# Two-block fp32 transformer on one core: keys rotated ahead of a score reading in three head steps, and another order of the first transfers and products

## The reference

```python
h = rmsnorm(x, norm_g)                      # gain norm_g, 1024 wide
proj = h @ w_in                             # queries, keys, values, gates of three branches
# branch A: 4 heads, each the difference of two softmaxes over causal scores (head width 64)
# branch C: 8 heads of width 64, windowed; for 512 tokens with dilations 1, 4, 16, merged by their lse
q, k = partial_rope(q), partial_rope(k)     # first 16 of 64 columns are rotated
s = einsum(q, k) * 64 ** -0.5;  p = softmax(mask(s));  o = p @ v
# branch B: gelu, layernorm, causal token mixing
x = x + (sum over branches of sigmoid(gate) * (y_branch @ w_branch)) @ w_out
```

## Time and profile before

| | us |
|---|---|
| median of 3 runs | 2323.68 |
| lowest, highest | 2322.32, 2325.24 |
| the profiled execution, its own time | 2325.3 |
| its span (first to last instruction) | 2323.5 |
| TensorE busy | 2308.4 |
| VectorE busy | 1481.2 |
| ScalarE busy | 978.6 |

### The profile page before, as it was taken

How to read it: one execution, slowest core, us unless ns; L and a number is a source line. 1 busy time by engine, 2 the same in 40 slices (tenths; PEclk the granted TensorE clock), 3 DMA queues, 4 the chain that set the end, 5 groups by cost and what they waited for, 6 DMA issues and landing times.

```text
span 2323.5 us, 30126 instructions
## 1 busy us (share of the span) xinstructions
PE 2308.4 (99%) x11442; PEld 1881.9 (81%) x11442; DVE 1481.2 (64%) x2781; ACT 978.6 (42%) x1811; POOL 0.2 (0%) x4
## 2 busy tenths in 40 slices
PE   9999999999999999999999999999999999999998
PEld 6888888888888878888877788888887768888887
DVE  6788763435478784444587668566567777658565
ACT  5356542223446553222567543232336764323222
POOL 0000000000000000000000000000000000000000
PEclk9999999999999999999999999999999999999999
DMA  4333334333243333233221133314313112422322
GB/s 167 107 105 105 104 96 112 92 99 100 84 117 109 97 103 114 93 100 117 65 88 55 56 127 102 127 55 145 118 37 97 55 46 100 145 82 91 127 64 99
DMA packets 74766, 226.84 MB, mean 98 GB/s; under 512 B 15296, under 2 KB 16192, under 8 KB 73856
## 3 DMA queue, kind: packets, MB, share of 16 engines
q1 hardware_dynamic: 74336, 224.14, 30.9%
q10 hardware_dynamic: 288, 0.79, 0.1%
HBM read 205.36 MB, written 2.10 MB: 89 GB/s over the span
## 4 chain that ended last, share of the span: by engine, by line
PE 96%; DVE 2%; ACT 1%; issue 0%; DMA 0%; DVEq 0%; SPq 0%
PE bank L590 25%; PE bank L592 25%; PE bank L591 25%; PE bank L2235 2%; PE bank L2237 2%; PE bank L2236 2%; PE bank L1310 2%; PE bank L2054 1%; PE bank L2013 1%; PE bank L1294 1%; PE bank L2038 1%; PE bank L524 1%; PE bank L1283 1%; PE bank L1281 1%; PE bank L2067 1%; PE bank L2096 0%
## 5 line engine op out<-in xcount | busy, mean ns | idle before, releaser
L590 PE MATMUL bank<-h_hi,w_hi 128*128 128x512 f32 x1984 | 784.7, 396 | 0.7 <-DVE sz L1769 0.3
L592 PE MATMUL bank<-h_lo,w_hi 128*128 128x512 f32 x1984 | 773.4, 390 | 0.0
L591 PE MATMUL bank<-h_hi,w_lo 128*128 128x512 f32 x1984 | 773.0, 390 | 0.0
L1157 DVE TENSOR_TENSOR w_lo<-raw_w,w_hi 128x1024 fp32r<-128x1024 f32 x314 | 378.9, 1221 | 97.4 <-ACT w_hi L1145 94.1
L590 PEld LDWEIGHTS bank<-h_hi,w_hi 128*128 128x128 f32 x1984 | 372.7, 188 | 82.5 <-issue 8.3
L592 PEld LDWEIGHTS bank<-h_lo,w_hi 128*128 128x128 f32 x1984 | 372.4, 188 | 79.8
L591 PEld LDWEIGHTS bank<-h_hi,w_lo 128*128 128x128 f32 x1984 | 372.9, 188 | 72.1
L1145 ACT ACTIVATE w_hi<-raw_w 128x1024 fp32r<-128x1024 f32 x314 | 327.6, 1054 | 159.5 <-DMA raw_w<-w_dram 159.1
L2472 ACT ACTIVATE nrm<-bank 128x512 f32<-128x512 f32 x44 | 26.4, 599 | 288.4 <-PE bank L592 288.4
L1611 ACT ACTIVATE ext<-bank 128x512 f32<-128x512 f32 x48 | 28.7, 598 | 274.3 <-PE bank L592 274.3
L1918 DVE TENSOR_TENSOR rope_a<-ext,bank 128x512 f32<-128x512 f32 x32 | 22.0, 688 | 165.8 <-PE bank L592 109.7
(11 more groups left out here) (372 smaller groups left out, 3504.6 us busy)
## 6 DMA issues: line engine op xcount, KB each, us to landing
raw_w<-w_dram SPq DMA_DIRECT2D x312, 512.0 KB, 3.6
down_raw<-w_dram SPq DMA_DIRECT2D x36, 512.0 KB, 4.5
extra_raw<-w_dram SPq DMA_DIRECT2D x10, 512.0 KB, 4.6
k_lo<-k_lo SPq DMA_DIRECT2D x32, 128.0 KB, 2.3
ln_row<-row_dram SPq DMA_DIRECT2D x4, 1024.0 KB, 6.6
last_raw<-w_dram SPq DMA_DIRECT2D x8, 512.0 KB, 4.6
rowp<-row_dram SPq DMA_DIRECT2D x2, 1024.0 KB, 11.9
rot_t<-raw_t SPq DMA_DIRECT2D x128, 16.0 KB
```

Of the source, the lines that this page charges most:

```text
L590: nc.tensor.matmul(dst, lh, rh, start=start, stop=False)
L591: nc.tensor.matmul(dst, ll, rh, start=False, stop=False)
L592: return nc.tensor.matmul(dst, lh, rl, start=False, stop=stop)
L1157: nc.vector.tensor_tensor(lo_of(u), raw_of(u), hi_of(u).bitcast(F32), ALU.subtract) \
```

## The change

Three things. In the steps of the joined heads 4 to 6, VectorE rotates the keys of the next head directly behind its queries, in (a, 1), ahead of the reading of the scores of (a, 2). In (a, 2) nothing is left between the split and `normalise` but the reading of bank O. Head 3's epilogue in (5, 1) then stands behind both rotations. At the start, token block 0 is loaded by SyncE as its third transfer and no longer by ScalarE's queue. And the gain diagonal is made by one instruction and not by two, TensorE makes two full products of zeros ahead of the sums (one and a half before) and none between the sums and the transposes (one before).

```diff
@@ -983,8 +983,7 @@
             sp.dma_start(const[:, 0:2 * P], const_in[:, 0:2 * P]).then_inc(ident_loaded, 16)
             sp.dma_start(colp[:, 0:P1_SUBLN], col_in[0, :, 0:P1_SUBLN]).then_inc(norm_loaded, 16)
             for tb in range(NB):
-                if tb:
-                    sp.dma_start(x[:, tb, :], x_in[tb * P:(tb + 1) * P, :]).then_inc(x_loaded[tb], 16)
+                sp.dma_start(x[:, tb, :], x_in[tb * P:(tb + 1) * P, :]).then_inc(x_loaded[tb], 16)
                 if tb < 2:
                     load(tb)
             load(2)
@@ -1161,18 +1160,17 @@
 
         def gain_sums(pe):
 
+            pe.wait_ge(gain_diag_ready, 1)
             diag = gain_diag[:, :, :].rearrange("p k c -> p (k c)")
             for c in range(2):
-                pe.wait_ge(gain_diag_ready, c + 1)
                 nc.tensor.matmul(T[c][:, :], ones, diag[:, SEQ * c:SEQ * (c + 1)], start=True, stop=True).then_inc(gain_summed, 1)
 
         def gain_diagonal(dve):
 
             dve.wait_ge(norm_loaded, 16)
-            for c in range(2):
-                nc.vector.tensor_tensor(gain_diag[:, 4 * c:4 * c + 4, :], ident.unsqueeze(1).to_broadcast([P, 4, P]),
-                                        colp[:, P1_NORM + 4 * c:P1_NORM + 4 * c + 4].unsqueeze(2).to_broadcast([P, 4, P]),
-                                        ALU.mult).then_inc(gain_diag_ready, 1)
+            nc.vector.tensor_tensor(gain_diag[:, :, :], ident.unsqueeze(1).to_broadcast([P, KD, P]),
+                                    colp[:, P1_NORM:P1_NORM + KD].unsqueeze(2).to_broadcast([P, KD, P]), ALU.mult) \
+              .then_inc(gain_diag_ready, 1)
 
 
         def tensor_block1(pe, layer):
@@ -1190,16 +1188,14 @@
 
             if layer == 0:
 
-                def zero_products(n, cols=SEQ):
+                def zero_products(n):
                     for _ in range(n):
-                        nc.tensor.matmul(O[:, 0:cols], ytmp[:, 0:P], ytmp[:, 0:cols], start=True, stop=True)
+                        nc.tensor.matmul(O[:, :], ytmp[:, 0:P], ytmp[:, :], start=True, stop=True)
 
                 pe.wait_ge(zeros_ready, 1)
-                zero_products(1)
-                zero_products(1, SEQ // 2)
+                zero_products(2)
                 pe.wait_ge(ident_loaded, 16)
                 gain_sums(pe)
-                zero_products(1)
                 entry_transpose(pe, e, 0, hn[0], (0,))
                 zero_products(2)
                 v_block(0, 0)
@@ -1418,8 +1414,6 @@
 
         def scalar_block1(act, st, layer):
             at, n0, e = Counts(names, layer), layer * B1_UNITS, ENTRY1[layer]
-            if layer == 0:
-                act.dma_start(x[:, 0, :], x_in[0:P, :]).then_inc(x_loaded[0], 16)
             nc.scalar.preload_act_table_set("natural_log_exp_and_others")
             def lam_exps():
                 act.wait_ge(lam_exp, at(lam_exp, 1))
@@ -1889,20 +1883,25 @@
                         split_to(dve, n0 + B1_HEADS + 6)
                     elif fill_of(*before):
                         split_to(dve, n0 + head_unit(*fill_of(*before)) + 3)
+                    if qb == 2 and a in JOINED1 and a > N_A:
+                        dve.wait_ge(y_ready, at(y_ready, 3 + a))
+                        epilogue(a - 1, False)
+                    if qb in (1, 2) and a in JOINED1:
+                        normalise(a, qb)
+                    if before in ROTATE1 and not (a in JOINED1 and qb == 2):
+                        rotate(*ROTATE1[before])
                     if second1(a, qb):
-                        normalise(a, qb)
-                    if before in ROTATE1:
-                        rotate(*ROTATE1[before])
+                        rotate(*ROTATE1[a, qb])
                     if (a, qb) in EPILOGUE1:
                         if qb:
-                            dve.wait_ge(qk_ready, at(qk_ready, 2 * a + 3))
+                            dve.wait_ge(qk_ready, at(qk_ready, 2 * a + 4))
                         epilogue(EPILOGUE1[a, qb])
-                    elif qb == (2 if a in JOINED1 else 1) and a > N_A:
+                    elif qb == 1 and a > N_A and a not in JOINED1:
                         epilogue(a - 1, False)
                     elif qb == 3 and a > N_A:
                         split_y(8 + a - 1 - N_A)
                         dve.wait_ge(y_ready, at(y_ready, 4 + a))
-                    if not second1(a, qb):
+                    if qb not in (1, 2) or a not in JOINED1:
                         normalise(a, qb)
                     if qb == (2 if a in JOINED1 else 1) and 1 <= a <= N_A:
                         split_squares(a - 1)
```

## The result

| | before | changed |
|---|---|---|
| median of 11 runs, us | 2323.68 | 2328.29 |
| lowest, highest | 2322.32, 2325.24 | 2325.95, 2330.2 |
| profiled execution, its span | 2325.3, 2323.5 | 2328.41, 2326.6 |

The ratio is 1.0018, with a 95% interval of 1.0010 to 1.0025: the change made the kernel slower, by 4.6 us between the medians (4.3 between the means). That is at the edge of what the prediction called the same, and 1 us above its range.

What follows compares the result with a forecast made beforehand. TensorE was taken as the bound, busy 2308.4 of 2323.5 us. Terms of +3.1, 0 and -2.4 made +0.7 us, so 2324.4 from the median 2323.68; range 2321.4 to 2327.3, the forecast's own 2322.8 to 2326.

Steps and rivals of the forecast that it cites:

- Term 1: Head step 5, both layers: scores of (5, 3) wait 2.7 us, the waits at `pv` go; +3.1 us, bounds +2.5 and +4.
- The new order does not by itself release O earlier: Head step 5: bank O is read at the same time as before, since the work ahead of it sums the same.
- Term 2: Head steps 4 and 6: the later reading of the scores has over 2 us to spare; 0 us.
- The exchange: Rival, head step 5: keys' exchange lands after the earlier rotation asks for it, VectorE stands; 2328.4 us, chance 0.05.
- Term 3: Program's start: gains land 1.3 us earlier, the product of zeros leaves the chain; -2.4 us, bounds +0.1 and -3.7.
- the first rival: Program's start: TensorE's clock rises earlier, by the second sum, saving 1.3 us; 2323.1 us, chance 0.25.
- The sum: Whole kernel: 3.1 - 2.4 = +0.7 us, time 2324.4, no change within 0.2%.

Runs made afterwards that it cites:

- twelve products: Changed kernel plus 12 unused products of 512 columns ahead of the scores of (5, 3), filling TensorE's wait: 2325.55 us.
- keys alone: Kernel before with only VectorE's new order in the head steps, start as before: 2330.32 us, ratio 1.0029.
- three products more: Changed kernel plus 3 unused products of 512 columns ahead of the scores of (5, 3), leaving 2.04 us idle: 2327.19 us.
- transfer alone: Kernel before with only token block 0 loaded by SyncE as its third transfer: 2322.07 us.
- start alone: Kernel before with only the start's changes, VectorE's order in the head steps as before: 2321.98 us, ratio 0.9992.

## Why the prediction was wrong

*Term 1, "Net: 3.0 - 1.47 = 1.5 us slower", +3.1 for both layers.* Here it failed. The wait was right in its place, its releaser and its size (2.7 forecast, 2.71 measured), and the waits of `pv` and the transposes went as said. But the sum went on at the full clock behind the wait. The fall of TensorE's clock was put at nothing: it cost 1.6 us in each layer by the timelines, 2.7 to 3.3 in all by the run with twelve products. Measured, term 1 is +6.1 by the keys alone, and 6.5 by the timelines of the changed kernel, of which 3.3 are the waits (3.1 forecast) and 3.2 the clock. Its bounds of +2.5 and +4 came from lengths of waits alone. The kernel before had a row that seemed to speak for that, an idle time of 1.28 us without a fall, but the new wait was twice as long. The prediction used the clock at the start and never asked for it here.

The Trainium skill ("TensorE: Matmul & The Clock Gate", section "HAM oscillation — how this bites in real kernels") says that idle gaps between matmuls bring the slow level back, in a kernel with longer gaps than these. The trace agrees, and has the fall already behind 2.71 us, and behind 2.04 with three products more.

*"The new order does not by itself release O earlier"*: right, O was read at the same time but for the start's gain. *Term 2, steps 4 and 6 at 0*: right, by the run that leaves only them. The exchange was no later than before (VectorE waits 4.2 us in four places for it in both kernels), and the keys' earlier start brought nothing.

*Term 3, -2.4 for the start*: right in size by the medians, -2.3, but in part by luck, since the parts were off. The gains came 1.9 us earlier, not 1.3, and the clock rose within the sums, as the first rival had it, in the profiled execution. So the two profiles differ by 3.4. Against that, the kernel before had been profiled with a start 1.2 us slower than the run with the keys alone had it. Token block 0 landed 0.8 us later than before. The prediction called that hidden, and in the profile of the changed kernel it is, barely: the statistics end at 7.20 and VectorE's copy of the gains at 7.25. TensorE's 0.7 us before the transposes are the way over that copy and the scaling, for which the sum had no place once the product of zeros was gone. In the start alone, where the sums came earlier, the late block cost 0.5 us.

*The sum.* 6.1 - 2.3 = 3.8 against the 0.7 forecast; measured as a whole 4.6, within what two medians scatter. None of the rivals named the fall, and the forecast's own range ended at 2326. The forecast was no change within 0.2%. The loss is 0.18 to 0.2%, and since the interval of the ratio begins at 1.0010, it is a real one.

## What to carry to other kernels

Price a new wait of TensorE twice, by its length and by the clock that may fall behind it. If the wait can't be taken away, products that nobody needs can be cheaper than an idle engine: six of them won 3.1 us here. Moving a long block of work ahead of an instruction that another engine waits for is to be judged by all that then stands before it: here the rotation alone was free, and the epilogue behind it made the wait. And a small transfer that the first computation needs is best issued with no large transfer of another queue beside it.

## What the runs showed of the hardware

- TensorE's clock fell behind idle times of 2.71 us (both layers of the changed kernel) and 2.04 us (both layers, three products more), and not behind 1.28, 1.37 and, once, 2.81 us. The length alone does not decide; what else does is not shown. How long it stayed low differed as well: the granted clock of the same stretch was 0.87 in one profile and 0.76 in another.
- The start of before, with the same instructions in two kernels, ran 1.2 us apart in two profiled executions (first weight product at 13.59 and 12.40), by the clock's rise.
- 4 KB in small packets landed 1.9 us after their issue when no large transfer of another queue ran beside them (changed kernel, and the transfer alone), and 3.8 us with one (before).
